# Hybrid encoder block on one core: another order of VectorE's and ScalarE's work in the q, k and v stage

## What is computed

```python
def rmsnorm(x, g):
    xf = x.astype(jnp.float32)
    y = xf * lax.rsqrt(jnp.mean(xf * xf, axis=-1, keepdims=True) + EPS)
    return (y * g.astype(jnp.float32)).astype(x.dtype)
...
        q = (rmsnorm(c_q, q_latent_g[l]) @ w_uq[l]).reshape(B, T, MLA_HEADS, QK_DIM)
        kv = (rmsnorm(c_kv, kv_latent_g[l]) @ w_ukv[l]).reshape(B, T, MLA_HEADS, QK_NOPE + V_DIM)
        k_nope, v = kv[..., :QK_NOPE], kv[..., QK_NOPE:]
        k_rope = jnp.broadcast_to(k_pe[:, :, None, :], (B, T, MLA_HEADS, QK_ROPE))
        k = jnp.concatenate([k_nope, k_rope], axis=-1)
        q = rmsnorm(q, q_norm_g[l])
        k = rmsnorm(k, k_norm_g[l])
        q = jnp.concatenate([q[..., :QK_NOPE], rope(q[..., QK_NOPE:], pos)], axis=-1)
        k = jnp.concatenate([k[..., :QK_NOPE], rope(k[..., QK_NOPE:], pos)], axis=-1)
        y_mla = block_attention(q, k, v).reshape(B, T, MLA_HEADS * V_DIM)
```

## Time and profile before

| | before |
|---|---|
| median of 3 runs | 1483.11 us (1481.14 to 1483.87) |
| the profiled execution | 1479.96 us, span 1478.2 us |
| TensorE matmul / weight load busy | 1381.7 us (93%) / 1155.2 us (78%) |
| VectorE busy | 728.7 us (49%), 1002 instructions |
| ScalarE busy | 528.1 us (36%), 698 instructions |
| GpSimd busy | 240.5 us (16%), 133 instructions |
| mean granted clock of TensorE | 0.96 of full speed |
| the q, k and v stage | first squares of q at 209.8 us, attention's first matmul at 268.5 us |

### The profile page before, as it was taken

One profiled execution on the slowest core, in us unless ns is written; L12 is line 12 of the kernel. 1 busy time (PEld: TensorE's weight loads), 2 busy tenths in 40 slices (PEclk: granted clock), 3 DMA queues, 4 the chain that ended last, 5 costly groups with the idle time before them and its releaser, 6 DMA issues.

```text
span 1478.2 us, 17247 instructions
## 1 busy us (share of the span) xinstructions
PE 1381.7 (93%) x6918; PEld 1155.2 (78%) x6918; DVE 728.7 (49%) x1002; ACT 528.1 (36%) x698; POOL 240.5 (16%) x133
## 2 busy tenths in 40 slices
PE   6989996599999999699799999999999999999998
PEld 5988985466666667478698889898888889898886
DVE  6767747577777762555523333434243333434243
ACT  6567632266676662534331202121211112021200
POOL 0000123200000000243231213032121213031200
PEclk9999998799999996799899999999999999999999
DMA  5101100000000004110121101020211101020103
GB/s 194 51 26 45 55 1 0 1 1 9 8 9 9 8 18 170 51 34 24 50 79 43 57 28 57 28 85 14 71 43 43 57 28 57 28 85 14 43 1 114
DMA packets 21094, 64.32 MB, mean 44 GB/s; under 512 B 5442, under 2 KB 6146, under 8 KB 18228
## 3 DMA queue, kind: packets, MB, share of 16 engines
q1 hardware_dynamic: 20676, 63.36, 12.4%
q10 hardware_dynamic: 368, 0.27, 0.1%
HBM read 59.20 MB, written 4.23 MB: 43 GB/s over the span
## 4 chain that ended last, share of the span: by engine, by line
PE 50%; DVE 0%; ACT 0%; issue 0%; DVEq 0%
PE banks L100 17%; PE banks L101 17%; PE banks L102 17%; DVE a_l L1870 0%; DVE ffn_act L1866 0%; ACT a_h L1832 0%; DVE h L1879 0%; DVEq L1865 0%
## 5 line engine op out<-in xcount | busy, mean ns | idle before, releaser
L100 PE MATMUL banks<-hn_h,up_h 128*128 128x342 f32 (+1 forms) x880 | 308.7, 351 | 1.7 <-PEq L1486 1.7
L101 PE MATMUL banks<-hn_l,up_h 128*128 128x342 f32 (+1 forms) x880 | 308.3, 350 | 0.0
L102 PE MATMUL banks<-hn_h,up_l 128*128 128x342 f32 (+1 forms) x880 | 307.8, 350 | 0.0
L100 PEld LDWEIGHTS banks<-hn_h,up_h 128*128 128x128 f32 x880 | 166.7, 189 | 17.2 <-POOL up_l L1512 1.8
L101 PEld LDWEIGHTS banks<-hn_l,up_h 128*128 128x128 f32 x880 | 166.8, 190 | 15.4
L102 PEld LDWEIGHTS banks<-hn_h,up_l 128*128 128x128 f32 x880 | 166.5, 189 | 15.7
L1879 DVE TENSOR_TENSOR h<-banks,h 128x512 f32<-128x512 f32 x176 | 121.7, 691 | 114.7 <-PE banks L102 114.7
L100 PE MATMUL banks<-dn_h,a_h 128*128 128x512 f32 x352 | 137.7, 391 | 3.7 <-DVE a_l L1870 3.7
L102 PE MATMUL banks<-dn_h,a_l 128*128 128x512 f32 x352 | 137.6, 391 | 0.0
L101 PE MATMUL banks<-dn_l,a_h 128*128 128x512 f32 x352 | 137.6, 391 | 0.0
L1797 POOL TENSOR_TENSOR dn_l<-dn_raw,dn_h 128x1024 fp32r<-128x1024 f32 x22 | 52.9, 2403 | 480.4 <-ACT dn_h L1830 480.4
(11 more groups left out here) (257 smaller groups left out, 2499.5 us busy)
## 6 DMA issues: line engine op xcount, KB each, us to landing
up_raw<-in_w_up SPq DMA_DIRECT2D x22, 1024.0 KB, 4.9
dn_raw<-in_w_down SPq DMA_DIRECT2D x22, 512.0 KB, 3.5
win_raw<-in_w_in SPq DMA_DIRECT2D x11, 512.0 KB, 3.3
x_tm<-in_x_tm SPq DMA_DIRECT2D x8, 512.0 KB, 4.3
wo_raw<-in_w_out SPq DMA_DIRECT2D x16, 256.0 KB, 4.5
h<-in_x_tm SPq DMA_DIRECT2D x8, 512.0 KB
out<-h SPq DMA_DIRECT2D x16, 256.0 KB, 2.0
sum_recip<-recip SPq DMA_DIRECT2D x7, 256.0 KB, 3.3
```

What stands on the lines that cost most here:

```text
L100: nc.tensor.matmul(out, w_h, x_h, start=first, stop=False)
L101: nc.tensor.matmul(out, w_h, x_l, start=False, stop=False)
L102: return nc.tensor.matmul(out, w_l, x_h, start=False, stop=last)
```

## The change

Tile i-1 is no longer scaled inside tile i. Each tile is now done to its end before the next tile's rope products: rope products, sum of q's squares, sum of k's squares, head variances, the low half of v (a function of its own, `low_v`, taken out of `scale`), then reciprocal, q and k. On ScalarE the root of tile i stands behind the high half of v of the same tile, ahead of the next tile's squares of q. The semaphore "kv_read", with which TensorE is told that the k and v banks are free, is now raised by k's product, which has become their last reader, and no longer by the low half of v. No instruction is added or taken away, and none changes its shape.

```diff
                 nc.scalar.activation(qsq[0:n].rearrange("p (b h) d -> p b (h d)", b=2), q_ps(i)[0:n], ACT.Square)\
                   .then_inc(sem["q_squares"], 1)
-                if i:
-                    head_std(i - 1)
                 act.wait_ge(sem["kv_mm"], i + 1)
...
                 nc.scalar.activation(vt[:, :, VD:2 * VD], kv_heads(i)[0:n, :, NOPE:], ACT.Copy, scale=r_kv[0:n, i:i + 1])\
                   .then_inc(sem["v_hi"], 1)
-            head_std(NT - 1)
+                head_std(i)
...
+            def low_v(i):
+                n = rows(i)
+                dve.wait_ge(sem["v_hi"], i + 1)
+                vt = v[0:n, i, :].rearrange("p (h d) -> p h d", h=HEADS)
+                nc.vector.scalar_tensor_tensor(out=vt[:, :, 0:VD], in0=kv_heads(i)[0:n, :, NOPE:], scalar=r_kv[0:n, i:i + 1],
+                                               in1=f32(vt[:, :, VD:2 * VD]), op0=ALU.mult, op1=ALU.subtract)
+
             def scale(i):
...
-                r = r_kv[0:n, i:i + 1]
                 x = qk[0:n, i, NQ:].rearrange("p (h d) -> p h d", d=QK)[:, :, 0:NOPE]
                 rk = st[:, 40:48].unsqueeze(2).broadcast_to((n, HEADS, NOPE))
-                nc.vector.scalar_tensor_tensor(out=x, in0=kv_heads(i)[0:n, :, 0:NOPE], scalar=r, in1=rk,
-                                               op0=ALU.mult, op1=ALU.mult)
-                dve.wait_ge(sem["v_hi"], i + 1)
-                vt = v[0:n, i, :].rearrange("p (h d) -> p h d", h=HEADS)
-                nc.vector.scalar_tensor_tensor(out=vt[:, :, 0:VD], in0=kv_heads(i)[0:n, :, NOPE:], scalar=r,
-                                               in1=f32(vt[:, :, VD:2 * VD]), op0=ALU.mult, op1=ALU.subtract)\
-                  .then_inc(sem["kv_read"], 1)
-
-            for i in range(NT + 1):
-                if i < NT:
-                    rope_parts(i)
-                    sum_q(i)
-                if i:
-                    scale(i - 1)
-                if i < NT:
-                    sum_k(i)
-                    head_var(i)
+                nc.vector.scalar_tensor_tensor(out=x, in0=kv_heads(i)[0:n, :, 0:NOPE], scalar=r_kv[0:n, i:i + 1], in1=rk,
+                                               op0=ALU.mult, op1=ALU.mult).then_inc(sem["kv_read"], 1)
+
+            for i in range(NT):
+                rope_parts(i)
+                sum_q(i)
+                sum_k(i)
+                head_var(i)
+                low_v(i)
+                scale(i)
```

## The result

| | before | after |
|---|---|---|
| median | 1482.12 us (4 runs, 1474.7 to 1483.87) | 1461.95 us (4 runs, 1458.41 to 1464.32) |
| profiled execution | 1479.96 us, span 1478.2 us | 1464.26 us, span 1462.4 us |
| TensorE matmul busy | 1381.7 us (93%) | 1374.9 us (94%) |
| VectorE busy | 728.7 us (49%) | 728.3 us (50%) |
| ScalarE busy | 528.1 us (36%) | 527.3 us (36%) |

The ratio of the runs is 0.9873, with a 95% interval of 0.985 to 0.9897: between 15 and 22 us faster. Three more comparisons on other occasions gave 0.9903 (0.9878 to 0.9928), 0.9875 (0.9849 to 0.9901) and 0.9898 (0.9878 to 0.9919). Over all 22 executions of the changed kernel the median is 1465.0 us. Two executions, one of the kernel before (4862.75 us) and one of the kernel with the rope products as cover (3667.01 us), were slow as a whole, and the ratios and medians leave them out.

What follows compares the result with a forecast made beforehand. The q, k and v stage was taken as bound by engines waiting in turn; 4.65 us a tile would save 15.4 us, from 1479.96 to 1464.5, or 1467.7 from the median; middle 1466 us, range 1463 to 1472.

Steps and rivals of the forecast that it cites:

- the first case: The main forecast for the q, k and v stage: engines stop waiting in turn, at full clock; chance 0.80.
- the ring: q, k and v stage: squares await TensorE (28.7 us), rope products await squares (15.1), TensorE awaits q product (14.5).
- the turns: q, k and v stage: TensorE, ScalarE and VectorE work one after another despite two bank sets, 5.86 us once round.
- The period: VectorE's list in the q, k and v stage, summed from start-to-start distances, was to take 4.65 us a tile.
- the new pair: Second variance to low half of v on VectorE, shown by no row: taken as 0.13 us, at most about 0.25.
- Rival 2: VectorE's neighbouring instructions in the stage overlap nothing: 0.58 us more per tile, 5.2 in nine, 1471 us; chance 0.03.
- The root's cover: Low half of v on VectorE hides ScalarE's root before the reciprocal, with 0.29 us to spare; otherwise a bare wait per tile.
- The places: Stage timeline: tile 1's rope product at 215.44, tile 8's at 248.0, stage end at 252.7 us, attention's start following.
- The clock: TensorE at full speed in all the stage's tiles, idling 1.1 of 4.65 us; attention's start unchanged, 2 us either way.
- rival 1: TensorE's clock still falls in the stage: 1.77 us per half-clock tile, 1469.5 to 1473, all seven 1478.4; chance 0.12.
- The sum: Stage ends at 252.7 instead of 268.15 us: 15.4 us gained, 12.9 between rope products, the rest in the tail.
- half of 3.15 us: Whole kernel: median lay 3.15 us above the profiled execution; 1466 us was taken as the middle of 1464.5 and 1467.7.

Runs made afterwards that it cites:

- the kernel with the rope products as cover: Changed kernel with the rope products, instead of the low half of v, between variances and reciprocal, low half last; median 1466.8 us, ratio to before 0.9918.
- the placed version: Changed kernel with low half of v on GpSimd, rope products behind the variances, GpSimd's subtraction held until the tile's variances are done; median 1460.9 us (10 runs).

## Why the prediction was right

The forecast was the first case, that the ring opens at full clock, and each of its steps can be held against a row. The one number outside is the median itself: 1461.95 us in that comparison lies 1 us below the forecast's 1463 to 1472, and the 22 executions together, at 1465.0, lie within.

- *What bounds the stage.* The ring of three waits was the right reading. Putting the turns back by one number in TensorE's wait made the stage 75.3 us; moving only reciprocal and q product opened it; ScalarE's order without VectorE's changed nothing. That the q product's place is what closes the ring was shown by the run that moved only it and the reciprocal, without which it can't be made.
- *The period.* 4.65 us from distances of the old order, 4.65 measured in seven of seven tiles. The assumed 0.13 for the new pair was 0.14. Rival 2, VectorE without overlap, is out: neighbours still start 0.08 to 0.09 before the end of the one ahead. The exception is the q product, which waits for the reciprocal's result and starts 0.03 after its end; it did so in the earlier trace rows already, where the prediction wrote "every neighbour". The Trainium skill, "VectorE: DVE Perf Modes", "The DRAIN you can't avoid", also says that a next operation that isn't held starts earlier, which the prediction left out; the rows here agree with that part, so the section doesn't speak for the rival.
- *The root's cover.* 0.36 us predicted bare, 0.38 a tile measured when the low half of v was taken away from there.
- *The places.* Tile 1's rope product was to come 1.3 us later than before and tile 8's near 248, attention's matmuls near 253: they came at 215.35, 247.88 and 252.91. From attention's first matmul to its first wait for a DMA it took the same 18.5 us, where 2 us either way had been allowed.
- *The clock.* Assumed full for all tiles, and full in all four profiles of the change, so rival 1 (0.12) didn't come about in any of them; why the clock stayed up was not tried. TensorE's idle time of 1.1 us a tile was mis-summed: its own numbers give 4.65 - 3.79 = 0.86, and 0.90 was measured. No term of the sum used it. The 15.4 us hold the old tiles at their average of 6.68, so the clock that the turns had cost is in the sum without a price of its own; by the estimate above it is 5.7 of the 15.5 us.
- *The sum.* 15.4 us for the stage by the rows. Measured there: 58.7 - 43.2 = 15.5. The point of 1466 us lay 4 above the median of that comparison and 1 above the median of all 22 executions. That the first four runs lay lower is put down to the spread of the rest of the program, which is argued and not shown, as only the profiled one of them has a trace: its stage is the same as in the three other profiles, and the two profiled executions, before and after, differ by 15.7 us in all.

The step that was weak is the last, half of 3.15 us taken off for a part of the difference between profile and median that "would go with the ring". In the one profile of before and the one of ScalarE's order alone, with VectorE's turns in both, the stage takes 58.7 and 59.0 us, though the clock falls come in another sequence. No run shows anything in the stage that could have gone, and that the middle came out nearer than 1467.7 is luck.

## What to carry to other kernels

Where two sets of buffers exist and the engines still take turns, look for the instruction that frees a buffer standing in its engine's list behind work for the next tile; moving that one instruction (here it and the reciprocal it needs, two of eleven) brought 12.0 of the 15.5 us, and ScalarE's order 0.3. The new period can be summed from start-to-start distances in the old trace, with any hand-over that becomes bare; here it held to a few hundredths of a microsecond. Then the engine with the longest list is the bound, and before some of it is moved to GpSimd, check what VectorE does with data in SBUF at that moment.

## What was not expected of the hardware

**A small VectorE instruction held by GpSimd.** A TENSOR_SCALAR over 8 values, with data and result in SBUF, lasted to the end of a GpSimd TENSOR_TENSOR that had begun before it, up to 1.19 us instead of 0.22; with the subtraction held back until it was done, it was at 0.21 to 0.23 in all nine tiles. The sum of k (0.68 us) and the reciprocal (0.25), with data and result in SBUF too, and the products that read PSUM (0.28 to 0.69) were not held beside the same subtraction. The Trainium skill, "SBUF — State Buffer", "Who interferes with whom", says that `tensor_scalar` can enter a mode that takes the pair of ports VectorE shares with GpSimd, and that whoever comes second waits for the whole instruction; the two end times, 0.02 to 0.03 us apart, agree. That the mode was entered isn't shown by any row. The variances also read a second operand from SBUF, one value per partition, which the sum and the reciprocal don't, so whether the kind of instruction or that operand made the difference stays open.

**Where the spread comes from.** The stage takes the same time to 0.1 us in all four profiles of the change, and in both of the placed version, while the rest ranges from 1204.4 to 1211.7 us with no edit in it. Two profiles with nearly equal stages and rests of 1210.2 and 1204.4 us differ mainly in one place, around the end of attention. By stretch, first the change (the profile with 1210.2), then the kernel with the rope products as cover:

```profile
540.00:560.00 20.00, 19.86 (x81) 16.52 (x82) 4.10 (x7) 4.17 (x5) 0.00 (x0) 0.59 0.79 305
560.00:580.00 20.00, 16.17 (x55) 10.83 (x53) 4.30 (x8) 6.08 (x7) 0.00 (x0) 0.65 0.01 1
```

```profile
540.00:560.00 20.00, 20.00 (x103) 16.64 (x102) 4.10 (x7) 6.12 (x7) 0.00 (x0) 0.76 0.79 299
560.00:580.00 20.00, 9.87 (x32) 5.51 (x30) 5.44 (x9) 4.15 (x5) 0.00 (x0) 0.67 0.05 14
```

In the first 20 us the one with the higher granted clock (0.76 against 0.59) gets 103 matmuls done against 81, and attention's last matmuls of q_h and k_h start at 564.0 against 570.1, some 6 us earlier. At which moment the clock falls and rises there differs between executions; why was not tried. Single executions of the changed kernel lie up to 11 us apart (1458.41 to 1469.23), more than the 4.8 us that the placed version gains in the stage, which is why one comparison with five runs of it didn't show that.
